# Two unused tensors around the weight ring in SBUF: 16 bytes before it, 48 bytes behind it

## The reference, cut to what matters

```python
def swiglu_ffn(x, w_gu, w_down):          # 1024 -> 2 x 2816 -> 1024, eight times
    gate, up = jnp.split(x @ w_gu, 2, axis=-1)
    return (jax.nn.silu(gate) * up) @ w_down
...
    for layer in range(DEPTH):
        x = x + 0.5 * swiglu_ffn(rms_norm(x, ffn1_norm[layer]), ffn1_w_gu[layer], ffn1_w_down[layer])
        ...
        x = x + memory_cross_attention(...)
        x = x + 0.5 * swiglu_ffn(rms_norm(x, ffn2_norm[layer]), ffn2_w_gu[layer], ffn2_w_down[layer])
```

## The kernel before, in words

| tensor | bytes per partition | start | start modulo 64 |
|---|---|---|---|
| raw | 16384 | 16512 | 0 |
| w_hi | 24576 | 32896 | 0 |
| w_lo | 24576 | 57472 | 0 |
| x | 8192 | 82048 | 0 |
| rcol_x | 8 | 175232 | 0 |
| rcol_m | 8 | 175264 | 32 |
| sil | 2048 | 175296 | 0 |
| a | 16384 | 179392 | 0 |
| b | 16384 | 195776 | 0 |

## Time and profile before

### The profile page before, as it was taken

One profiled execution on the slowest core, in us unless ns is written; L12 is line 12 of the kernel. 1 busy time (PEld: TensorE's weight loads), 2 busy tenths in 40 slices (PEclk: granted clock), 3 DMA queues, 4 the chain that ended last, 5 costly groups with the idle time before them and its releaser, 6 DMA issues.

```text
span 2692.8 us, 51716 instructions
## 1 busy us (share of the span) xinstructions
PE 2612.7 (97%) x18604; PEld 2409.3 (89%) x18604; DVE 1919.6 (71%) x3131; ACT 1502.7 (56%) x2579; POOL 201.3 (7%) x280
## 2 busy tenths in 40 slices
PE   8999799999999999999999999999999999999998
PEld 7998689999998899999998998989989999988997
DVE  7777676778777576777777667777777776676876
ACT  6556556556555656556555555655565565555554
POOL 0001001000000201000000160000000005300000
PEclk9999899999999999999999999999999999999999
DMA  7654244655554344555654542445545545335553
GB/s 257 202 190 137 79 141 149 226 203 187 188 187 157 98 161 134 188 187 167 207 186 139 184 157 95 163 158 185 187 157 186 185 146 170 128 118 165 172 187 109
DMA packets 122821, 445.80 MB, mean 166 GB/s; under 512 B 13688, under 2 KB 14712, under 8 KB 122688
## 3 DMA queue, kind: packets, MB, share of 16 engines
q1 hardware_dynamic: 120816, 436.79, 48.7%
q0 software_dynamic: 1872, 7.17, 0.7%
HBM read 442.86 MB, written 1.05 MB: 165 GB/s over the span
## 4 chain that ended last, share of the span: by engine, by line
PE 93%; DVE 5%; ACT 2%; issue 1%; DMA 0%; SPq 0%; DVEq 0%; ACTq 0%
PE bank L454 92%; DVE w_lo L1468 1%; PE bank L805 1%; DVE rt L1696 1%; DVE z L1534 1%; ACT w_hi L1034 0%; DVE rt L1490 0%; DVE x L1527 0%; DVE a L1495 0%; ACT score L1268 0%; DVE rstd_x L1487 0%; DMA raw<-in_stream_dram 0%; ACT L1242 0%; DVE z L1824 0%; DVE z L1827 0%
## 5 line engine op out<-in xcount | busy, mean ns | idle before, releaser
L454 PE MATMUL bank<-a,w_hi 128*128 128x256 f32 (+1 forms) x5360 | 1342.3, 329 | 39.3 <-DVE a L1495 38.6
L1468 DVE TENSOR_TENSOR w_lo<-raw,w_hi 128x1024 fp32r<-128x1024 f32 x829 | 1016.3, 1230 | 279.5 <-ACT w_hi L1034 278.4
L454 PE MATMUL bank<-a,w_lo 128*128 128x256 f32 x3736 | 1013.1, 282 | 0.0
L454 PEld LDWEIGHTS bank<-a,w_hi 128*128 128x128 f32 x5360 | 897.4, 190 | 127.2 <-issue 45.8
L1034 ACT CAST w_hi<-raw 128x1024 fp32r<-128x1024 f32 x829 | 857.1, 1045 | 44.5 <-DMA raw<-in_stream_dram 35.4
L454 PE MATMUL bank<-b,w_hi 128*128 128x256 f32 (+1 forms) x4096 | 859.3, 301 | 4.2 <-DVE b L1495 3.2
L454 PEld LDWEIGHTS bank<-a,w_lo 128*128 128x128 f32 x3736 | 709.2, 190 | 16.7
L454 PEld LDWEIGHTS bank<-b,w_hi 128*128 128x128 f32 x4096 | 656.9, 188 | 41.2 <-issue 3.6
L454 PE MATMUL bank<-b,w_lo 128*128 128x256 f32 x2400 | 658.5, 280 | 0.0
L454 PEld LDWEIGHTS bank<-b,w_lo 128*128 128x128 f32 x2400 | 450.5, 188 | 5.6
L1077 ACT COPY pt<-bank 128x256 f32<-128x256 f32 x176 | 65.5, 372 | 219.1 <-PE bank L454 219.1
(11 more groups left out here) (185 smaller groups left out, 2128.7 us busy)
## 6 DMA issues: line engine op xcount, KB each, us to landing
raw<-in_stream_dram SPq DMA_DIRECT2D x829, 512.0 KB, 3.3
z<-in_biasc_dram POOLq DMA_DIRECT2D x6, 512.0 KB, 4.5
z<-in_biasa_dram POOLq DMA_DIRECT2D x3, 512.0 KB, 4.4
x<-in_x_dram SPq DMA_DIRECT2D x2, 512.0 KB, 8.1
v<-in_mem_dram POOLq DMA_DIRECT2D x2, 512.0 KB, 4.9
out_dram<-x SPq DMA_DIRECT2D x8, 128.0 KB, 1.9
con<-in_con_dram POOLq DMA_DIRECT2D x1, 912.0 KB, 6.3
vec<-in_vec_dram POOLq DMA_DIRECT2D x1, 417.0 KB, 5.8
```

What stands on the lines that cost most here:

```text
L454: return nc.tensor.matmul(out, lhsT, rhs, start=start, stop=stop, skip_group_check=shared)
L1468: return nc.vector.tensor_tensor(out, a, hi.bitcast(F32), ALU.subtract)
```

## The change

Two tensors are declared that nothing uses: `gap_w`, 4 fp32 words (16 bytes) per partition, between `raw` and `w_hi`, and `gap_x`, 12 words (48 bytes), between `w_lo` and `x`. In the words that go with the change, the weight ring lies 16 bytes further, at the remainder modulo 64 that the activation buffers have, and all other tensors keep their remainders. No instruction is written differently.

```diff
         raw = sb("raw", [P, RAW, D])
+        sb("gap_w", [P, 4])
         w_hi = sb("w_hi", [P, RING, D], F32R)
         w_lo = sb("w_lo", [P, RING, D], F32R)
+        sb("gap_x", [P, 12])
         x = sb("x", [P, C, T])
```

## The result

The changed kernel takes 2709.73 us in the median (2707.27 to 2711.31), beside 2693.56 us for the kernel before. The recorded ratio is 1.0053, 95% interval 1.004 to 1.0066; the two medians by themselves would give 1.0060. So the change costs some 14 to 16 us, about three times the 5.4 us that count as no change here, and the time lies above the range that was given (2685 to 2703 us).

The account below looks back on a forecast made before the run. The prediction took TensorE's stream of matmuls to bound the kernel. Its terms, 0 + 0 + 0 on the profiled 2694.85 us, gave a forecast median of 2693.1 us, range 2685 to 2703 us, with 0.73 for no difference.

Parts of the forecast that it names:

- What bounds the kernel: Whole kernel: TensorE's stream of matmuls sets the time, with 93% of the chain that ended last; DMA has nothing.
- What is really moved: Buffer addresses: with rounding to 32 bytes, ring and activations go together from remainder 0 to 32 modulo 64; raw stays.
- rival D: Addresses: packed without rounding, the ring would come to equal the activations' remainder; no chance of its own, counted within A and B.
- TensorE, 17,080 times 0: Matmuls reading the ring: spacing change taken as 0, between 4.3 ns less and 7.4 ns more for each of 17,080.
- Rival A: Ring matmuls: slow spacings turn fast, 20.6 us to 2672.5 us, or 2644 us with feed-forward blocks; chance 0.11.
- Rival B: Ring matmuls outside the feed-forward blocks: 1,877 fast distances turn slow, 8.1 us, to 2701.2 us; chance 0.07.
- the signs of being wrong: Down-tile spacing moving over 0.3 ns, or TensorE waiting for w_lo; slowed fast stretches would show B.
- My upper bound of 2703 us: Top of the forecast range for the whole kernel, set to reach over B's 2701.2 us.
- Rival C: All 17,080 ring matmuls: starts off a 64-byte boundary cost up to 7.4 ns each, 126 us, 2819 us; chance 0.09.
- ScalarE, VectorE, loads: Casts and subtractions: at most 17 and 20 ns more each, hidden, so 0; loads 0, since raw doesn't move.
- The rule of the Trainium skill: TensorE's operand reads: independent ports would force 0; left unused against A and B, as it leaves 4.3 ns unexplained.

Follow-up runs that it names:

- e4_ring16_rest64: Against the kernel before: starts allowed at multiples of 16, ring 16 bytes further, everything behind it 64 bytes further; 2716.64 us, ratio 1.0075.
- e2_all32: Against the kernel before: all tensors, raw included, 32 bytes further, every distance between them unchanged; 2694.8 us, ratio 0.9997.
- e9_rest256: Against the kernel before: ring at its old place, everything behind it 256 bytes further; 2694.36 us, ratio 0.9998.
- e12_act192: Against the kernel before: only a, b and the small tensors behind them 192 bytes further, distance 0; 2721.98 us, ratio 1.0097.
- e5_rest128: Against the kernel before: ring at its old place, everything behind it 128 bytes further, distance 192; 2673.42 us, ratio 0.9917.
- e10_nosplit: Against the changed kernel: from the seventh weight tile on, ScalarE and VectorE split only 4 of 1024 columns; 2700.99 us.

## Why the prediction was wrong

- **What bounds the kernel**: right. Some 15 of the 16.1 us of loss are in the distances between neighbouring ring matmuls of the mixers, and no other engine came onto the chain.
- **What is really moved**: right, and it decided the reading. By its words the change would have given distance 112 and 2717 us (e4_ring16_rest64). Compiled, it gave 128 and 2710 us. The time would have been forecast wrongly either way, but rival D would have sent the search after a remainder of 16.
- **TensorE, 17,080 times 0**: this is the step that failed. It rested on two reasons. The first was that both spacings stand side by side at unchanged addresses. That is true of the earlier trace rows and stays true: in e2_all32 and e9_rest256, at the old distance, some stretches of the mixers changed sides (`xa 0` is 1.9 and 2.7 us longer). But that something else also chooses between the spacings doesn't make the addresses harmless; they decide which spacings there are and how often each is taken. And the list of fast distances itself held a hint: its first row has the weights moving, and so have about half of the fast distances (950 of 1,924 of at most 115 ns), which lie at 192 and not at 64 by moving start less stationary start. So the trace of before did hold two relations of the addresses, against the prediction's word that no row shows what a change would do. The second was that the remainders modulo 64 stay equal. The modulus is 256, and by it the distance went from 64 to 128. I had worked out the shift of 64 bytes and used it only for rivals A and B. In the place of 0 the runs show 16.1 us / 17,080 = 0.94 ns per matmul, nearly all of it in the mixers. Of the signs of being wrong, that of rival B came: the stretch of the earlier trace rows is at 118.6 ns. The sign in a down tile came as well, but says little: the tile of the earlier trace rows went from 117.9 to 118.5 ns by unrounded starts, while over the feed-forward blocks the slow distances rose by 0.08 ns.
- **Rival B** had the sign, and its mechanism in the main: the fast distances turned slow. Its price was 1,877 x 4.3 ns = 8.1 us, and it was too small in two ways. The fast distances rose by 5.6 ns, to 118.95 and not to 117.6 (117.8 by unrounded starts), which made 10.5 us. And I had held the slow spacing for an upper end; there are slower ones, and 4,770 slow distances rose by 0.96 ns, 4.6 us. My upper bound of 2703 us was built on that.
- **Rival C** is excluded by e2_all32: remainder 32 for all operands, 2694.8 us.
- **Rival A** names something real, a stream that is more often in its fast spacing, but at distance 192, and its price was right by luck: 20.6 us forecast in the mixers, 22 us less measured. In the profiled execution (2677.85 us, the longest of the five) the span is 17.0 us shorter, 13.2 us of it in the feed-forward blocks and 3.3 us in the mixers.
- **ScalarE, VectorE, loads**: right; 1224 and 1042 ns, and no wait for `w_lo`.
- **The granted clock** is no cause. Its mean over the span is 0.984 in the changed kernel and 0.987 before, but 0.988 in the slow e12_act192 and 0.984 in the fast e5_rest128.
- **The rule of the Trainium skill** (SBUF — State Buffer, Who interferes with whom: TensorE's two read ports are independent, and TensorE waits for nobody). As for other engines, e10_nosplit agrees: 119.59 and 119.60 ns. As for TensorE's own two operands the measurement speaks otherwise, and decides: their distance alone is worth from -22 to +27 us. That I didn't use the rule to exclude A and B was right; that I still gave 0.73 to no change was not.

What stays open is the mechanism below the distance. That the two read streams meet in SBUF is argued from the modulus and from e10_nosplit, and not shown. Nor do the runs tell why the best distance is 192, or what sets a stretch at an unchanged distance to one of its patterns.

## What to carry to other kernels

In a kernel whose TensorE stream has no cover, the distance between the buffer of the weights and that of the activations is a parameter of its own: here eleven distances, all multiples of 16 bytes, gave 2673 to 2723 us from the same instructions. Read the distances between starts, not mean durations; if one form runs at two spacings, or its distances form a repeating pattern, put padding between the two buffers and measure several distances modulo 256, apart for matmuls whose weights are stationary and those whose weights move. And read the addresses from the compiled program: the tensors one declares for padding may be rounded up, and what moves is then something else than was meant.

## What the runs showed of the hardware that I had not expected

- The spacing of fp32r matmuls of 256 columns depends on the start of the moving operand less that of the stationary one, modulo 256 bytes: 113.3 ns at best, 120.0 ns throughout a tile at distance 0. It doesn't depend on where both lie together (2694.8 us with all tensors moved by 32 bytes).
- Two distances can share their spacings and differ in how often each is taken: at 64 and at 192 the matmuls of the mixers run at 113.3 or 117.8 ns, with 18% against 70% at 114 ns and less where the weights are stationary.
- It is sharp: 2673 us at distance 192, 2711 and 2713 us at 176 and 208.
- Taking nearly all of VectorE's and ScalarE's work at the ring away changed the spacing by 0.01 ns in the feed-forward blocks.
- A pattern that suits the 256-column matmuls need not suit those of 512 columns: at distance 192 the former gained up to 2.9 ns and the latter lost 2.4 ns.
